# A cross attention's second input, loaded a second time as columns instead of being turned on TensorE

## The chip, the cores and the metric

The kernel runs on one NeuronCore of a Trainium2 chip. Its time is the device time of one execution in microseconds (us); less is better. All arithmetic is in float32, in places split in two float32r parts, as told below.

## The reference, cut to what matters

Two transformer layers follow each other on 256 rows of 1024 numbers. The second has a cross attention whose keys and values come from a second input `mem` (256 rows of 1024 numbers), not from the running rows. Only this part is touched:

```python
def _rmsnorm(x, g):
    x32 = x.astype(jnp.float32)
    y = x32 * lax.rsqrt(jnp.mean(x32 * x32, axis=-1, keepdims=True) + EPS)
    return y.astype(x.dtype) * g

def _cross_attention(hn, memn, wq, wkv, wo):
    B, L, _ = hn.shape
    q = (hn @ wq).reshape(B, L, X_HEADS, X_HEAD_DIM)
    kv = memn @ wkv
    k, v = jnp.split(kv, 2, axis=-1)
    k = k.reshape(B, N_MEM, X_HEADS, X_HEAD_DIM)
    v = v.reshape(B, N_MEM, X_HEADS, X_HEAD_DIM)
    s = jnp.einsum('bshd,bmhd->bhsm', q.astype(jnp.float32), k.astype(jnp.float32)) * (X_HEAD_DIM ** -0.5)
    p = jax.nn.softmax(s, axis=-1)
    o = jnp.einsum('bhsm,bmhd->bshd', p.astype(v.dtype), v).reshape(B, L, X_W)
    return o @ wo
...
    h = h + _cross_attention(_rmsnorm(h, norm_x_g[l]), _rmsnorm(mem, norm_mem_g[l]),
                             wx_q[l], wx_kv[l], wx_o[l])
```

The norm of a row of `mem` is a factor of that row (one number for each of the 256 rows) times a gain for each column. The keys and the values are linear in the normed row, so the row's factor can be put on `mem` or on the finished keys and values.

## The kernel before, in words

**Weights.** Every matrix product streams its weights from HBM in units of 128 x 1024 numbers (512 KB). SyncE's queue (SP) loads a unit into one of five buffers `raw`; ScalarE (ACT) rounds it to float32r in `whi` (line 940, through `make_hi`); VectorE (DVE) puts the rest, raw less hi, in `wlo` (line 1452, `make_lo`); TensorE (PE) multiplies hi by hi, lo by hi and hi by lo into PSUM (`pb`), three matmuls for each product. Each of `raw`, `whi` and `wlo` has five buffers. `make_hi` of a unit waits until PE is done with the unit five before it, the load of a unit waits for `make_lo` of the unit five before it. PE takes 12 matmuls of 512 columns for a unit of the form `rows`, and 24 of 256 columns for one of the form `cols`.

**Order.** Each engine has a program of its own, written out by hand; semaphores tie them together. `run(name, side, ...)` of ACT and DVE makes the units of one weight group and after each unit takes one step of the side programs given to it, which hold the work that does not follow the stream of weights. PE's `rows` and `cols` do the same: behind each unit comes one step of a side program. The groups in question, in order: `b1_wa`, `b1_wb` (branches of the first layer), `b1_wo` (its output product), `f1_up`/`f1_dn` (its feed forward), then `mk` and `mv` (keys and values of the cross attention, from `mem`), then `b2_cg0` and what follows in the second layer. The side program `turn_block1` runs beside `b1_wb1`, `b1_wo0`, `b1_wo1` and the first `f1_up`.

**mem.** SP waits until the first layer's attention is done (`pv_done`), since `MEM` lies where that attention's tiles were, and then loads `MEM`, 256 rows as two tiles of 128 rows. ACT squares and sums the rows (line 985), DVE makes the mean (`mean`, lines 1482 and 1484), GpSimd (POOL) the factor by a power (line 2144), and DVE multiplies the rows by it (`norm_rows`, line 1494: four instructions of 512 columns). In `turn_block1` PE turns the scaled rows into columns: `turn_tiles(T_MEM, j, MEM, ...)` for j = 0 to 3, four 128 x 128 transposes each (line 418 is the source of each transpose, line 414 of each matmul), into PSUM bank 4 + j. ACT copies them with the gain into `OT` (a part of `ZO`) rounded to float32r, DVE puts the rest beside it (line 1511). Much later `mk` makes the keys, columns of `KXT`, and `mv` the values, `VX`, which ACT copies out of PSUM; the cross attention uses both.

The first layer's own input takes another way, with lines that the change uses again: its factor is put on a diagonal (`DR`, line 1946), one matmul of `ones` with it spreads the factors over all partitions, and DVE copies them to `RX` (line 1950).

Of the kernel before, what the change touches and what calls it, by code (L numbers as in the profile page):

```python
# [8 lines left out]
F32 = mybir.dt.float32  # L9
F32R = mybir.dt.float32r  # L10
ALU = mybir.AluOpType
# [3 lines left out]
P = 128  # L15
# [24 lines left out]
POW = {n: i for i, n in enumerate((N_X, N_MEM, N_MIX, N_XA, N_END))}  # L40

END_PARTS = (((0, 1, 0, 512), (1, 1, 512, 1024)), ((0, 2, 0, 320), (1, 2, 640, 1024), (0, 3, 320, 640)))
SCALED = {n: i for i, n in enumerate((N_MEM, N_MIX))}
GAIN = {T_X: "norm1", T_MEM: "normmem", T_2: "norm2", T_MIX: "normmix", T_XA: "normx", T_FFN: "normffn"}
PE_CONV = 5

# [1 line left out]
def build(nc, A, out):  # L48
    ctx = ExitStack()
    with ctx:  # L50
# [54 lines left out]
        DR = work(W0 + 15224, "DR", 256)  # L105
        RX = work(W0 + 18296, "RX", 256)
        MEM = work(W0 + 10480, "MEM", 2048)
        MSQ = work(W0 + 8192, "MSQ", 1024)
        RT = work(W0 + 8704, "RT", 512)[:, :].rearrange("p (i n) -> p i n", i=2)
        HF = work(W0 + 9216, "HF", 1024)[:, :].rearrange("p (i n) -> p i n", i=4)  # L110
# [171 lines left out]

        x_in, mem_in = [sem("x_landed0"), sem("x_landed1")], [sem("mem_landed0"), sem("mem_landed1")]
        xt_in, gain_in = [sem(f"x_columns_landed{i}") for i in range(3)], sem("first_gain_landed")
        dr_made, rx_done, rx_out = sem("factor_diagonals"), sem("factor_rows"), sem("factor_rows_copied")
        cst_in, prm_in, cb_in, wc_in = sem("consts_landed"), sem("params_landed"), sem("consts2_landed"), sem("wcmp_landed")
        zeros, first_in, first_k = sem("zeros_made"), sem("first_k_tile_landed"), sem("first_k_tile_made")
# [59 lines left out]
        def sync_program(e):  # L347
# [28 lines left out]
            for u in range(NRAW, NU):  # L376
                if u == 8:
                    e.dma_start(WC, A["wcmp"].rearrange("p (w j e) -> p w j e", w=2, j=16)).then_inc(wc_in, 16)
                if u == 12:
                    e.dma_start(CB[:, :], A["consts2"]).then_inc(cb_in, 16)  # L380
                if u == b1 + 46:
                    e.wait_ge(pv_done, 16)
                    for t in range(2):
                        e.dma_start(MEM[:, t * D:t * D + D], memv[:, t, :]).then_inc(mem_in[t], 16)
                for k, (at, name) in enumerate(((48, "b2_q1"), (58, "b2_gc0"), (62, "b2_gc1"), (66, "b2_ga0"))):
                    if u == b2 + at:
                        e.wait_ge(*out_at[name, 3 if k == 0 else 1])
                        src = A["b_gate_2"][:, 512 * k:512 * k + 512].broadcast_to([P, 512])
                        e.dma_start(BG[:, :], src).then_inc(bg_in, 16)
                if u == b2 + 28:  # L390
                    e.wait_ge(*out_at["b2_ca1", 3])
                    e.wait_ge(u4_zero, 1)
                if b2 + 28 <= u < b2 + 32:
                    j = u - b2 - 28
                    a = 1 if j == 0 else 0
                    for g in range(4):
                        e.dma_start(U4[32 * j:32 * j + 32, :, g, a:284],
                                    U2[32 * g:32 * g + 32, PE_CONV:8, j + a - 1:j + 283]).then_inc(u4_in, 16)
                if u == f2 + 24:
                    e.wait_ge(xv_done, 4)  # L400
                    e.dma_start(GF[:, :], A["norm_final_g_2"].broadcast_to([P, D])).then_inc(gf_in, 16)
                e.wait_ge(lo, u - NRAW + 1)
                load(u)
# [8 lines left out]
        def tensor_program(e):  # L412
# [122 lines left out]
                for _ in steps:  # L535
                    pass

            def rows_scaled(n, j):
                e.wait_ge(scaled, 4 * SCALED[n] + 2 * (j // 2) + 2)

            def factor_rows():
                yield
# [6 lines left out]
            def turn_block1():  # L549
                yield  # L550
                for j in range(2):
                    e.wait_ge(mixed, 2)
                    turn_tiles(T_M1, j, GB)
                    yield
                yield
                for j in range(2, 4):
                    e.wait_ge(mixed, 4)
                    turn_tiles(T_M1, j, GB)
                yield
                for j in range(4):  # L560
                    rows_scaled(N_MEM, j)
                    turn_tiles(T_MEM, j, MEM, (t_lo, t_at[T_M1, j]))
                    yield
                for j in range(2):
                    e.wait_ge(*out_at["b1_wo0", 1])
                    turn_tiles(T_2, j, X, (t_lo, t_at[T_MEM, j]))
                    yield
                yield
                for j in range(2, 4):
                    e.wait_ge(*out_at["b1_wo1", 1])  # L570
                    turn_tiles(T_2, j, X, (t_lo, t_at[T_MEM, j]))
                yield

            def turn_mix():
                for _ in range(3):
                    yield
                for j in range(4):
                    rows_scaled(N_MIX, j)
                    turn_tiles(T_MIX, j, XS, out_at[f"f1_dn7_{j // 2}", j % 2])
                yield  # L580

# [293 lines left out]
            def cross_scores(h):  # L875
                o = PB[4 + h]
                e.wait_ge(t_lo, t_at[T_XA, h])
                e.wait_ge(*out_at["xq", h])
                for t in range(2):
                    i = mm(o[:, 256 * t:256 * t + 256], QX[:, h, t * P:t * P + P], KXT[:, h, :], t == 0, t == 1)  # L880
                i.then_inc(xs_done, 1)
# [50 lines left out]
        def scalar_program(e):  # L932
# [56 lines left out]
                return XS[:, t * D + 512 * i:t * D + 512 * i + 512]  # L989

            def make_t_hi(s, j, T):
                e.wait_ge(turned, 4 * (s - 1) + j + 1)
                if s in GAIN:
                    for k in range(2):
                        kt = 2 * j + k
# [6 lines left out]
            def turn_block1():  # L1002
# [6 lines left out]
                for j in range(2, 4):  # L1009
                    make_t_hi(T_M1, j, XT)  # L1010
                yield
                for j in range(4):
                    make_t_hi(T_MEM, j, OT)
                    yield
                for j in range(2):
                    make_t_hi(T_2, j, XT)
# [316 lines left out]
                make_t_hi(T_MIX, j, XT)  # L1333
            run("mv")
            for t in range(2):
                copy_out("mv", t, VX[:, t, :])


            run("b2_cg0")
# [92 lines left out]
        def vector_program(e):  # L1432
# [85 lines left out]
                                    d[:, :, 0, :].bitcast(F32), ALU.subtract).then_inc(t_lo, 1)  # L1518

            def turn_block1():  # L1520
                yield
                yield
                for j in range(2):
                    make_t_lo(T_M1, j, XT)
                    yield
                yield
                for j in range(2, 4):
                    make_t_lo(T_M1, j, XT)
                yield
                for j in range(4):  # L1530
                    make_t_lo(T_MEM, j, OT)
                    yield
                for j in range(2):
                    make_t_lo(T_2, j, XT)
                    yield
                yield
                for j in range(2, 4):
                    make_t_lo(T_2, j, XT)
                yield
# [259 lines left out]
            def attention2():  # L1799
                for s in range(45):  # L1800
# [36 lines left out]
                        make_o_lo(h, 4 + h, 6)  # L1837
                    yield

            def conv_blocks():  # L1840
                for n in range(8 - PE_CONV):
                    e.tensor_tensor(WQ[n].rearrange("p q g c -> p (q g) c"),
# [142 lines left out]
            for i in range(2):  # L1985
                run(f"b1_wa{i}")
                times(f"b1_wa{i}", GA, i, gate_made(0))
            norm_rows(N_MEM, MEM, MEM)
            run("b1_wb0")
            times("b1_wb0", GB, 0, gate_made(2), N_X)  # L1990
            plus("b1_wb0", GB, 0, GA)
# [13 lines left out]
            run("mk")  # L2005
            for j in range(4):
                make_t_lo(T_MIX, j, XT)
            run("mv", conv_blocks())


            step(e.memset(U2[:, :, 0:30], 0.0))
# [244 lines left out]
```

## Time and profile before

| | |
|---|---|
| median of three runs | 939.59 us (939.23 to 940.73) |
| the profiled execution | 939.12 us, of which its span in the trace is 937.3 us |
| TensorE busy | 923.2 us (98% of the span) |
| VectorE busy | 681.2 us (73%) |
| ScalarE busy | 520.1 us (55%) |
| GpSimd busy | 14.9 us (2%) |
| read from HBM | 163.72 MB, 176 GB/s over the span |
| granted TensorE clock | 0.999 of full speed |

The profile is one execution. Its span runs from the first to the last instruction; the execution's own time is 1.8 us more. Busy time is the sum of instruction durations; a matmul's duration begins before the one ahead of it has ended, so the distance between the starts of two matmuls tells what one costs in a stream, and its duration does not.

### The profile page before, as it was taken

Reading aid. Unit: us, or ns where it says so; the run is one execution under the profiler, and the core shown is the slowest. Engines: PE = TensorE matmul, PEld = TensorE weight load, DVE = VectorE, ACT = ScalarE, POOL = GpSimd, SP = SyncE. Lnnn points to the kernel's source line nnn. Section 1 sums busy time; section 2 is a strip of 40 time slices with the busy share of each in tenths; the row PEclk is TensorE's granted clock in tenths of the full one; section 3 lists DMA queues with packets and bytes.
Section 4 is the critical chain, followed back from the end, with each engine's and each line's share of the span. In section 5 each row is a group of like instructions: output and inputs, shape, how many; then the busy total and the mean of one; then the engine's idle time right before and its main releaser. Section 6 shows DMA issues by size and latency. Waiting matters only on the chain.

```text
span 937.3 us, 14384 instructions
## 1 busy us (share of the span) xinstructions
PE 923.2 (98%) x5515; PEld 795.0 (85%) x5515; DVE 681.2 (73%) x1173; ACT 520.1 (55%) x880; POOL 14.9 (2%) x20
## 2 busy tenths in 40 slices
PE   8999999999999999999999999999999999999997
PEld 6898987788888888889999988887788888888886
DVE  5769975477776666667478989999786676666665
ACT  5745677745654444456444436654945664454553
POOL 0300000000000000000000000000000000000000
PEclk9999999999999999999999999999999999999999
DMA  9855444656565566554654945554465346655551
GB/s 347 284 151 155 136 139 133 201 186 183 172 204 196 185 188 193 185 198 141 208 161 142 248 136 154 171 173 155 157 229 175 94 159 222 214 189 180 180 180 45
DMA packets 89315, 167.51 MB, mean 179 GB/s; under 512 B 7648, under 2 KB 11808, under 8 KB 89120
## 3 DMA queue, kind: packets, MB, share of 16 engines
q1 hardware_dynamic: 89024, 166.53, 56.1%
q8 instruction: 44, 0.72, 0.3%
q14 instruction: 23, 0.19, 0.1%
q10 hardware_dynamic: 224, 0.07, 0.0%
HBM read 163.72 MB, written 1.05 MB: 176 GB/s over the span
## 4 chain that ended last, share of the span: by engine, by line
PE 92%; ACT 3%; DVE 2%; DMA 2%; issue 1%; SPq 0%; POOL 0%; POOLq 0%; DVEq 0%
PE pb L414 89%; PE pb L418 3%; DMA raw<-in_w_in 2%; ACT whi L940 1%; DVE wlo L1452 1%; ACT YC L1252 0%; DVE LNS L1878 0%; ACT XS L985 0%; ACT ZO L940 0%; ACT GA L1075 0%; ACT L1252 0%; ACT L1075 0%; DVE GA L1739 0%; DVE ST L1614 0%; ACT S L1389 0%
## 5 line engine op out<-in xcount | busy, mean ns | idle before, releaser
L1452 DVE TENSOR_TENSOR wlo<-raw,whi 128x1024 fp32r<-128x1024 f32 (+2 forms) x300 | 357.0, 1213 | 148.3 <-ACT whi L940 147.0
L940 ACT ACTIVATE whi<-raw 128x1024 fp32r<-128x1024 f32 (+2 forms) x302 | 309.8, 1045 | 164.3 <-PE pb L414 151.0
L414 PE MATMUL pb<-XT,whi 128*128 128x256 f32 (+1 forms) x1552 | 372.6, 323 | 1.3 <-issue 1.3
L414 PE MATMUL pb<-XT,wlo 128*128 128x256 f32 (+1 forms) x1032 | 290.5, 282 | 0.0
L414 PEld LDWEIGHTS pb<-XT,whi 128*128 128x128 f32 x1552 | 257.6, 190 | 29.6 <-issue 5.3
L414 PE MATMUL pb<-whi,ZO 128*128 128x512 f32 (+1 forms) x808 | 253.1, 390 | 0.4 <-DVE wlo L1452 0.4
L414 PEld LDWEIGHTS pb<-XT,wlo 128*128 128x128 f32 (+1 forms) x1032 | 195.8, 190 | 0.5
L414 PE MATMUL pb<-whi,XT 128*128 128x512 f32 (+1 forms) x544 | 176.4, 394 | 4.1 <-DVE wlo L1452 2.8
L414 PEld LDWEIGHTS pb<-whi,ZO 128*128 128x128 f32 x808 | 151.2, 188 | 33.1 <-DVE wlo L1452 1.6
L414 PE MATMUL pb<-wlo,ZO 128*128 128x512 f32 (+1 forms) x404 | 156.5, 387 | 0.0
L414 PEld LDWEIGHTS pb<-whi,XT 128*128 128x128 f32 x544 | 101.2, 188 | 26.7 <-DVE wlo L1452 4.3
L414 PE MATMUL pb<-wlo,XT 128*128 128x512 f32 (+1 forms) x272 | 103.2, 385 | 0.0
L414 PEld LDWEIGHTS pb<-wlo,ZO 128*128 128x128 f32 x404 | 75.9, 188 | 14.8
L1865 DVE SCALAR_TENSOR_TENSOR YC<-U,PR,YC 128x256 f32<-128x256 f32 x150 | 63.4, 477 | 0.0
L414 PEld LDWEIGHTS pb<-wlo,XT 128*128 128x128 f32 x272 | 51.3, 188 | 8.8
L940 ACT ACTIVATE RT<-pb 128x256 f32<-128x256 f32 x64 | 24.1, 376 | 40.5 <-PE pb L414 40.5
L1779 DVE TENSOR_TENSOR HF<-pb,RT 128x256 f32<-128x256 f32 x64 | 26.8, 418 | 24.8 <-ACT RT L940 24.8
L940 ACT ACTIVATE ZO<-HF 128x256 fp32r<-128x256 f32 x64 | 26.8, 418 | 24.9 <-DVE HF L1782 23.3
L1141 ACT ACTIVATE SM<-SM,ST 128x128 f32<-128x128 f32 (+1 forms) x48 | 21.4, 447 | 16.7 <-DVE ST L1593 16.7
L1782 DVE SCALAR_TENSOR_TENSOR HF<-HF 128x256 f32<-128x256 f32 x64 | 27.2, 425 | 2.2
L1771 DVE TENSOR_TENSOR ZO<-HF,ZO 128x256 fp32r<-128x256 f32 x64 | 26.8, 419 | 2.4 <-ACT ZO L940 0.6
L2144 POOL TENSOR_TENSOR ST<-ST,CST 128x1 f32<-128x1 f32 (+3 forms) x14 | 13.5, 971 | 917.9 <-DVE ST L1484 687.5
(220 smaller groups left out, 593.7 us busy)
## 6 DMA issues: line engine op xcount, KB each, us to landing
raw<-in_w_in SPq DMA_DIRECT2D x107, 512.0 KB, 3.7
raw<-in_w_ff SPq DMA_DIRECT2D x64, 512.0 KB, 4.5
raw<-in_w_up SPq DMA_DIRECT2D x32, 512.0 KB, 4.4
raw<-in_w_down SPq DMA_DIRECT2D x32, 512.0 KB, 4.6
raw<-in_w_branch_b SPq DMA_DIRECT2D x8, 512.0 KB, 4.8
raw<-in_w_out SPq DMA_DIRECT2D x8, 512.0 KB, 4.8
raw<-in_wx_kv SPq DMA_DIRECT2D x8, 512.0 KB, 4.2
raw<-in_w_attn_out SPq DMA_DIRECT2D x8, 512.0 KB, 3.4
```

The lines of the kernel that those rows point to most:

```text
L414: return e.matmul(o, l, r, start=start, stop=stop, skip_group_check=True)
L418: return e.transpose(o, s, ident[0:n, 0:n])
L940: return e.activation(o, i, ACT.Copy, scale=scale)
L1141: i = e.activation(SM[j % 4][:, c0:c1], SM[j % 4][:, c0:c1], ACT.Exp, bias=INM[j % 4][:, t:t + 1], scale=post, accum_out=ISM[j % 4][:, t:t ...
L1452: e.tensor_tensor(wlo[u % NW][:, 0:c], raw[u % NRAW][:, 0:c], whi[u % NW][:, 0:c].bitcast(F32), ALU.subtract).then_inc(lo, 1)
L1771: e.tensor_tensor(ZT[:, a + 256:a + 512], HF[:, f, :], ZT[:, a:a + 256].bitcast(F32), ALU.subtract).then_inc(h_lo, 1)
L1779: e.tensor_tensor(HF[:, f, :], PB[bank_of[name, f]][:, 0:256], RT[:, m % 2, :], ALU.add).then_inc(out_d, 1)
L1782: e.scalar_tensor_tensor(out=HF[:, f, :], in0=HF[:, f, :], scalar=0.0, in1=HF[:, f, :], op0=ALU.max, op1=ALU.mult).then_inc(h_sq, 1)
L1865: m = e.scalar_tensor_tensor(out=YC[:, f, :], in0=U2[:, f, k:k + 256], scalar=prm("convw2", 8 * k + f), in1=YC[:, f, :], op0=ALU.mult, op1 ...
L2144: return e.tensor_tensor(dst, src, mhalf(rows, n), ALU.pow)
```

## The change

`mem` is loaded once more, already turned by the host: `memt` holds its columns as rows of the tile `MT` (128 x 2048, 1 MB), which lies where the first layer's queries, keys and values were. SP issues this load between the same wait and the two loads of `MEM`. ACT and DVE read `MT` for the two parts of `OT`, with the gain and without the row's factor. `MEM` is still loaded for the squares; it isn't scaled and isn't turned any more. The row's factor now goes on the results: on the keys by a multiply in place (`scale_keys`, with the factors spread over partitions by one matmul and a copy to `RX`), on the values as the scale of ACT's copy out of PSUM. A table of turn numbers (`TURN`) replaces arithmetic, since one turn fewer is counted. The pieces below are, in order: the tile's place; SP's loads; PE's `turn_block1` and `cross_scores`; ACT's `turn_block1` and its copy behind `mv`; DVE's `turn_block1` (two pieces), the new `scale_keys`, and the calls ahead of `b1_wb0` and at `mv`.

```diff
+        MT = work(W0, "MT", 2048)
...
                 if u == b1 + 46:
                     e.wait_ge(pv_done, 16)
+                    e.dma_start(MT[:, :], A["memt"]).then_inc(mt_in, 16)
                     for t in range(2):
                         e.dma_start(MEM[:, t * D:t * D + D], memv[:, t, :]).then_inc(mem_in[t], 16)
...
-                for j in range(4):
-                    rows_scaled(N_MEM, j)
-                    turn_tiles(T_MEM, j, MEM, (t_lo, t_at[T_M1, j]))
-                    yield
+                e.wait_ge(t_lo, t_at[T_M1, 0])
+                e.wait_ge(dr_made, 4)
+                mm(PB[4][:, 0:256], ones, DR[:, :], True, True).then_inc(rx_done, 1)
+                for _ in range(4):
+                    yield
+                e.wait_ge(rx_out, 2)
                 for j in range(2):
                     e.wait_ge(*out_at["b1_wo0", 1])
-                    turn_tiles(T_2, j, X, (t_lo, t_at[T_MEM, j]))
+                    turn_tiles(T_2, j, X, (t_lo, t_at[T_M1, j]))
...
                 e.wait_ge(*out_at["xq", h])
+                e.wait_ge(kx_scaled, 4)
...
+                e.wait_ge(mt_in, 16)
+                e.wait_ge(*tile_at["b1_wa1", 1])
                 for j in range(4):
-                    make_t_hi(T_MEM, j, OT)
+                    for kt in (2 * j, 2 * j + 1):
+                        copy(OT[:, kt * 512:kt * 512 + 256], MT[:, kt * 256:kt * 256 + 256],
+                             prm(GAIN[T_MEM], kt)).then_inc(t_hi, 1)
                     yield
...
             for t in range(2):
-                copy_out("mv", t, VX[:, t, :])
+                e.wait_ge(factor, 2 * POW[N_MEM] + t + 1)
+                copy_out("mv", t, VX[:, t, :], NR[N_MEM][t])
...
+                for t in range(2):
+                    e.wait_ge(factor, 2 * POW[N_MEM] + t + 1)
+                    e.tensor_scalar(DR[:, t * P:t * P + P], ident, NR[N_MEM][t], None, ALU.mult).then_inc(dr_made, 1)
...
+                e.wait_ge(rx_done, 2)
+                e.tensor_copy(RX[:, :], PB[4][:, 0:256]).then_inc(rx_out, 1)
                 for j in range(4):
-                    make_t_lo(T_MEM, j, OT)
+                    for kt in (2 * j, 2 * j + 1):
+                        a = kt * 512
+                        e.wait_ge(t_hi, t_at[T_MEM, j] - 1 + kt % 2)
+                        e.scalar_tensor_tensor(out=OT[:, a + 256:a + 512], in0=MT[:, kt * 256:kt * 256 + 256],
+                                               scalar=prm(GAIN[T_MEM], kt), in1=OT[:, a:a + 256].bitcast(F32),
+                                               op0=ALU.mult, op1=ALU.subtract).then_inc(t_lo, 1)
                     yield
...
+            def scale_keys():
+                for f in range(4):
+                    e.wait_ge(*out_at["mk", f])
+                    if f == 0:
+                        e.wait_ge(rx_out, 2)
+                    e.tensor_tensor(KXT[:, f, :], KXT[:, f, :], RX[:, :], ALU.mult).then_inc(kx_scaled, 1)
+                    yield
...
-            norm_rows(N_MEM, MEM, MEM)
+            for t in range(2):
+                mean(N_MEM, t, 4 * N_MEM + 3 + t)
...
-            run("mv", conv_blocks())
+            run("mv", conv_blocks(), scale_keys())
```

Where PE turned `mem`, beside the product `b1_wo0`, its program of before reads as follows; `pb<-CST,MEM x4` is one `turn_tiles` of `mem`, the matmuls between are one weight unit:

```order
789 L414 MATMUL pb<-whi,XT 128x512
790 L418 MATMUL pb<-CST,MEM 128x128 x4
791 L414 MATMUL pb<-whi,XT 128x512
792 L414 MATMUL pb<-wlo,XT 128x512
...
799 L414 MATMUL pb<-whi,XT 128x512
800 L418 MATMUL pb<-CST,MEM 128x128 x4
```

The same place in the changed program (its line numbers are 4 higher); `pb<-DR,CST` is the one matmul that spreads the factors:

```order
789 L418 MATMUL pb<-whi,XT 128x512
790 L418 MATMUL pb<-DR,CST 128x256
791 L418 MATMUL pb<-whi,XT 128x512
792 L418 MATMUL pb<-wlo,XT 128x512
...
799 L418 MATMUL pb<-whi,XT 128x512 x2
800 L418 MATMUL pb<-wlo,XT 128x512
```

Of the four groups of four transposes none is left; one matmul stands at the place of the first, and the other three places hold nothing.

On DVE, the program of before around `mv`, behind `mk`; `wlo` is `make_lo`, `WQ` a table for the second layer's convolution, `U` a memset:

```order
341 L1452 TENSOR_TENSOR wlo<-raw,whi 128x1024
342 L1842 TENSOR_TENSOR WQ<-CST,PR 128x1024
343 L1452 TENSOR_TENSOR wlo<-raw,whi 128x1024
344 L1842 TENSOR_TENSOR WQ<-CST,PR 128x1024
345 L1452 TENSOR_TENSOR wlo<-raw,whi 128x1024
346 L1842 TENSOR_TENSOR WQ<-CST,PR 128x1024
347 L1452 TENSOR_TENSOR wlo<-raw,whi 128x1024
348 L2011 MEMSET U 128x8x30
349 L1452 TENSOR_TENSOR wlo<-raw,whi 128x1024 x8
```

The same place of the changed program:

```order
343 L1463 TENSOR_TENSOR wlo<-raw,whi 128x1024
344 L1873 TENSOR_TENSOR WQ<-CST,PR 128x1024
345 L1868 TENSOR_TENSOR KXT<-KXT,RX 128x256
346 L1463 TENSOR_TENSOR wlo<-raw,whi 128x1024
347 L1873 TENSOR_TENSOR WQ<-CST,PR 128x1024
348 L1868 TENSOR_TENSOR KXT<-KXT,RX 128x256
349 L1463 TENSOR_TENSOR wlo<-raw,whi 128x1024
350 L1873 TENSOR_TENSOR WQ<-CST,PR 128x1024
351 L1868 TENSOR_TENSOR KXT<-KXT,RX 128x256
352 L1463 TENSOR_TENSOR wlo<-raw,whi 128x1024
353 L1868 TENSOR_TENSOR KXT<-KXT,RX 128x256
354 L2043 MEMSET U 128x8x30
```

Three of the four multiplies of the keys now stand ahead of a `make_lo`, and one behind the last.

## Rows read from the trace of the kernel before

**Rows 1.** Page, busy time of each engine, and the chain by engine.

```profile
PE 923.2 (98%) x5515; PEld 795.0 (85%) x5515; DVE 681.2 (73%) x1173; ACT 520.1 (55%) x880; POOL 14.9 (2%) x20
...
PE 92%; ACT 3%; DVE 2%; DMA 2%; issue 1%; SPq 0%; POOL 0%; POOLq 0%; DVEq 0%
```

**Rows 2.** PE timeline, turns of mem: start us, us, engine, line, op, count.

```profile
223.79 0.60 PE L418 MATMUL pb<-CST,MEM 128*128 128x128 f32 x4
...
236.61 0.60 PE L418 MATMUL pb<-CST,X 128*128 128x128 f32 x4
```

**Rows 3.** PE timeline, a stretch of 114 matmuls with no turn.

```profile
184.30 0.62 PE L414 MATMUL pb<-whi,ZO 128*128 128x512 f32 x2
...
210.14 0.62 PE L414 MATMUL pb<-whi,ZO 128*128 128x512 f32 x2
```

**Rows 4.** PE timeline, a float32 matmul of ones inside the stream.

```profile
656.26 0.39 PE L414 MATMUL pb<-whi,ZO 128*128 128x512 f32 x1
656.49 0.59 PE L414 MATMUL pb<-LNS,CST 128*128 128x256 f32 x2
...
657.15 0.40 PE L414 MATMUL pb<-wlo,ZO 128*128 128x512 f32 x1
```

**Rows 5.** Groups by shape, 20-50 and 223.79-236.61 us: xcount, busy us, mean ns, idle.

```profile
L414 PE MATMUL pb<-DR,CST 128*128 128x256 f32 x2 | 0.6, 377 | 0.0
...
L1946 DVE TENSOR_SCALAR DR<-CST,ST 128x128 f32<-128x128 f32 x2 | 0.6, 286 | 0.1
...
L418 PE MATMUL pb<-CST,MEM 128*128 128x128 f32 x16 | 2.4, 272 | 0.0
```

**Rows 6.** DMA issues: KB each, median us to landing.

```profile
raw<-in_w_in SPq DMA_DIRECT2D x107, 512.0 KB, 3.7
...
MEM<-in_mem SPq DMA_DIRECT2D x2, 512.0 KB, 6.5
...
raw<-in_w_branch_b SPq DMA_DIRECT2D x1, 512.0 KB, 7.1
...
WC<-in_wcmp SPq DMA_DIRECT2D x1, 1024.0 KB, 11.1
```

**Rows 7.** SP and ACT timelines, loads of mem and their use.

```profile
177.83 0.82 SPq L384 DMA_DIRECT2D MEM<-in_mem  x2
179.33 13.51 SPq L356 DMA_DIRECT2D raw<-in_w_branch_b  x6
...
189.54 1.06 ACT L940 ACTIVATE whi<-raw 128x1024 fp32r<-128x1024 f32 x1 [1.66 <-PE pb L414]
190.51 0.61 ACT L985 ACTIVATE MSQ<-MEM 128x512 f32<-128x512 f32 x1
...
203.14 1.06 ACT L940 ACTIVATE whi<-raw 128x1024 fp32r<-128x1024 f32 x1 [1.66 <-PE pb L414]
```

**Rows 8.** DVE timeline, from the scaling to the diagonals' place.

```profile
196.54 1.84 DVE L1494 TENSOR_SCALAR MEM<-MEM,ST 128x512 f32<-128x512 f32 x4 [0.41 <-POOL ST L2144]
198.29 4.62 DVE L1452 TENSOR_TENSOR wlo<-raw,whi 128x1024 fp32r<-128x1024 f32 x4
...
207.67 3.49 DVE L1452 TENSOR_TENSOR wlo<-raw,whi 128x1024 fp32r<-128x1024 f32 x3
```

**Rows 9.** ACT, DVE and PE timelines, at mv.

```profile
440.35 1.06 ACT L940 ACTIVATE whi<-raw 128x1024 fp32r<-128x1024 f32 x1 [0.96 <-PE pb L414]
...
444.35 1.22 DVE L1452 TENSOR_TENSOR wlo<-raw,whi 128x1024 fp32r<-128x1024 f32 x1
...
445.53 0.40 PE L414 MATMUL pb<-XT,whi 128*128 128x256 f32 x2
...
446.60 0.40 PE L414 MATMUL pb<-XT,whi 128*128 128x256 f32 x2
```

**Rows 10.** Groups by shape, whole span: a DVE multiply of 256 columns.

```profile
L1724 DVE TENSOR_TENSOR CC<-pb,RX 128x256 f32<-128x256 f32 x8 | 2.8, 415 | 0.0
```

**Rows 11.** Page, PE's longest idle time with no releaser.

```profile
L414 PE MATMUL pb<-XT,whi 128*128 128x256 f32 (+1 forms) x1552 | 372.6, 323 | 1.3 <-issue 1.3
```

More of the change, by code:

```diff
@@ L42 @@
 END_PARTS = (((0, 1, 0, 512), (1, 1, 512, 1024)), ((0, 2, 0, 320), (1, 2, 640, 1024), (0, 3, 320, 640)))
-SCALED = {n: i for i, n in enumerate((N_MEM, N_MIX))}
+TURN = {s: i for i, s in enumerate((T_M1, T_2, T_MIX, T_M2, T_XA, T_FFN))}
 GAIN = {T_X: "norm1", T_MEM: "normmem", T_2: "norm2", T_MIX: "normmix", T_XA: "normx", T_FFN: "normffn"}
@@ L284, in build @@
         xt_in, gain_in = [sem(f"x_columns_landed{i}") for i in range(3)], sem("first_gain_landed")
+        mt_in, kx_scaled = sem("mem_columns_landed"), sem("cross_keys_scaled")
         dr_made, rx_done, rx_out = sem("factor_diagonals"), sem("factor_rows"), sem("factor_rows_copied")
@@ L536, in now, with rows_scaled @@
                     pass
-            def rows_scaled(n, j):
-                e.wait_ge(scaled, 4 * SCALED[n] + 2 * (j // 2) + 2)
+            def rows_scaled(j):
+                e.wait_ge(scaled, 2 * (j // 2) + 2)
             def factor_rows():
@@ L570, in turn_block1 @@
                     e.wait_ge(*out_at["b1_wo1", 1])
-                    turn_tiles(T_2, j, X, (t_lo, t_at[T_MEM, j]))
+                    turn_tiles(T_2, j, X, (t_lo, t_at[T_M1, j]))
                 yield
@@ L577, in turn_mix @@
                 for j in range(4):
-                    rows_scaled(N_MIX, j)
+                    rows_scaled(j)
                     turn_tiles(T_MIX, j, XS, out_at[f"f1_dn7_{j // 2}", j % 2])
@@ L991, in make_t_hi @@
             def make_t_hi(s, j, T):
-                e.wait_ge(turned, 4 * (s - 1) + j + 1)
+                e.wait_ge(turned, 4 * TURN[s] + j + 1)
                 if s in GAIN:
@@ L2242 @@
     xt = I["x"].reshape(256, 8, P).transpose(2, 1, 0).reshape(P, 2048)
-    arrays = {"xt": xt, "params": params, "consts": c, "consts2": c2, "wcmp": wcmp, "x": I["x"], "mem_2": I["mem_2"],
+    memt = I["mem_2"].reshape(256, 8, P).transpose(2, 1, 0).reshape(P, 2048)
+    arrays = {"xt": xt, "memt": memt, "params": params, "consts": c, "consts2": c2, "wcmp": wcmp, "x": I["x"], "mem_2": I["mem_2"],
               "b_gate_2": I["b_gate_2"], "norm_final_g_2": I["norm_final_g_2"].reshape(1, D)}
```

## The prediction

> **What bounds the kernel now.** I read the page first: PE is busy for 923.2 of 937.3 us, and the chain that ended last runs 92% through it, against 3% through ACT and 2% through DVE [rows 1]. So a microsecond taken off PE's stream is worth a microsecond, and work added to ACT, DVE or the loads is worth nothing until it makes PE wait. Then the timelines around the places that the change touches, to see two things: what the turned tiles of mem cost in the stream, and how far ahead of PE the other engines run there. In the stretch of the turns [rows 2] the rows carry no idle time ahead of any instruction of PE.
>
> **What PE loses.** Sixteen transposes, in four groups. From the first group's start to the start of the next turn behind the fourth is 236.61 - 223.79 = 12.82 us, for four units of twelve matmuls and four groups [rows 2]. The same matmuls without turns: 114 in 210.14 - 184.30 = 25.84 us, 0.2267 us each, so 2.72 us a unit and 10.88 us for four [rows 3]. The four groups cost 12.82 - 10.88 = 1.94 us, 0.49 us each, the slower start of the matmul behind each included.
>
> The transposes' own durations would give more: 272 ns each [rows 5], 4.35 us for 16. But each starts before the one ahead has ended, so I go by the distances, 1.94 / 16 = 0.12 us each. The Trainium skill, "TensorE: Matmul & The Clock Gate", section "Part 4: PE-mode transpose", gives about 275 ns for a 128 x 128 transpose in a kernel's context (measured in bf16); an estimate by it takes 16 x 0.275 = 4.4 us off PE where the distances take 1.94.
>
> **What PE gains.** One float32 matmul of ones with the diagonals, 256 columns. The trace has such a matmul, as two rows, inside the stream: the matmul ahead starts at 656.26, the second one behind at 657.15; two steps of 0.2267 from 656.26 would bring that start to 656.71 had the ones not been there, so they cost 0.44 us [rows 4]. Bounds: not below one step of the stream, 0.23 us; not above twice its busy time of 377 ns, 0.75 us [rows 5]. I take 0.44, the only one read in a stream of the same kind. PE also gets a wait on `kx_scaled` at each of four score products and one on `rx_out`; all are met long before (below). Such waits can't be priced from a row; I bound them by 0 and by 0.05 us each, a fifth of one matmul's step, so 0 to 0.25 us, and take 0, because a matmul that waits for several things that are done, the ones of [rows 4] among them, shows no more than its own cost.
>
> So PE's stream gets shorter by 1.94 - 0.44 = 1.50 us.
>
> **What lies beside it, and its cover.**
> *SP and the transfers.* The wait for `pv_done` is the same one; behind it MT, 1 MB, goes out ahead of MEM, and the loads of weights stand behind in the same queue. Before, MEM's two loads went out from 177.83 on and took 6.5 us (median), and the first load of weights behind them, at 179.33, took 7.1 us and landed at 186.4 [rows 6, 7]. One more issue on SP is 0.41 us (two took 0.82), and the next load went out 0.68 us behind those, so SP itself delays nothing. With MEM's 1 MB ahead the weights took 7.1 us where such a load commonly takes 3.7 [rows 6]: 3.4 us for 1 MB. I take the same for MT's 1 MB: MEM lands at 184.3 + 3.4 = 187.7, the weights at 189.8. Lower bound 0; upper bound the 11.1 us that the one other load of 1 MB took from issue to landing, near the kernel's start amid other loads [rows 6].
> What needs them: ACT's `make_hi` of those weights began at 189.54, when PE had freed the buffer, and the squares of MEM at 190.51 [rows 7]. So at 3.4 us ACT waits 0.3 us. PE wants that unit only four units later, at 189.54 + 4 x 2.72 = 200.4; ACT takes 1.06 and DVE 1.2 us for it, so its weights may land at 198.1, a delay of 11.7 us. The next unit's hi stands behind the squares on ACT, its lo behind the means on DVE, from 198.29 to 199.5; PE wants it at 203.1, a slack of 3.6 us, and 5.4 us once the 1.84 us of scaling ahead of it are gone [rows 8]. If DVE took up the means as soon as the squares are there, that path would break when these start at 190.5 + 5.4 = 195.9, a delay of MEM of 11.6 us. So even the upper bound is covered, by half a microsecond.
> *DVE beside b1_wb1.* Two diagonals, 0.57 us together [rows 5], stand behind the first of the three `make_lo`s from 207.67 on. That one's unit was freed for ACT at 203.14, the next one's 2.72 us later, so PE wants the next at 205.86 + 10.88 = 216.7; its lo was done at 207.67 + 2 x 1.16 = 210.0, now 210.6 [rows 7, 8]. Uncovered it would cost its 0.57 us. The factors from POOL were there at 196.5 [rows 8], more than 10 us earlier. Then one copy to RX, taken like the multiply of its size at 0.41 us [rows 10], ahead of the first rest of OT; uncovered again its 0.41. Before, DVE waited just there for ACT's copy of a turned tile; that copy now comes from MT and waits for no turn. PE wants `rx_out` four units later, 11 us on, and `dr_made` 15 us behind the diagonals.
> *DVE at mv.* Four multiplies of 256 columns at 0.415 us [rows 10], 1.66 us. Three stand ahead of the `make_lo` that began at 444.35. Its unit was freed for ACT at 440.35, so PE wants it four units later: two of mv are left behind the one that it then begins, and end when cg0 starts at 445.53; two units of cg0 (24 matmuls of 0.12 us, 2.88 us each) bring 451.3 [rows 9]. Lo was done at 445.57, now 1.25 us later at 446.8: 4.5 us are left. If that cover were gone the cost would be at most the 1.66 us. The loads that wait for these `make_lo`s go out up to 1.25 us later and land in some 4 us, into buffers that ACT wants only when PE has freed the unit five before, 10.9 us after `make_hi` of it could begin.
> *ACT.* As many copies, read from MT instead of PSUM. The two copies of the values get a factor as an operand instead of a constant; the banks that they free are wanted by the third and the fourth tile of cg0, not by the first, so a tenth of a microsecond there moves nothing.
>
> **Sum.** The profiled execution was 939.12 us, so 937.62 for such a one. The median of the runs is 0.47 us above it; I put the same on top: 938.1 us, 0.16% less. Before the end nothing brings the 1.5 us back: the later waits of PE are for engines that PE itself paces, so they move with it.
>
> **The rivals.**
> *Durations rule (faster).* If a transpose costs its duration, PE loses 4.35 us and gains 0.75 by the same rule: 3.6 us net, 936.0. For it speaks only the mean duration [rows 5]; against it the distances [rows 2, 3]. An estimate by the skill's 275 ns, in the page named above, is 4.4 - 0.44 = 4.0 us, 935.6. 5%.
> *A stall of code (either way).* PE has one gap of 1.3 us with no releaser anywhere [rows 11]. It lies ahead of the change, but PE's program is shorter behind it, and a gap of this kind could come or go. Gone, or the ones hidden to their lower bound together with a lucky median: 938.1 - 1.3 = 936.8, 12%. One more: 939.4, 13%, which with my sum is as good as no change.
> *The loads (slower).* MT ahead of MEM and the weights, in one queue. It decides from a delay of 11.7 us on (11.6 for MEM); each microsecond more is one of PE, first at the unit wanted at 200.4. Slower than before begins at 11.7 + 1.5 = 13.2 us; at 16 us it gives 938.1 + 4.3 = 942.4. For it: MEM and the weights behind already took 6.5 to 7.1 us where 3.7 is common. Against: 1 MB took at most 11.1 us, from issue to landing, amid the loads of the start [rows 6]. 4%.
> *It brings nothing because a wait takes its place.* PE would wait at T_2's turns for `rx_out`, or DVE for the ones: 939.6. Against: 11 us of slack. Within the 13% above.
>
> **How the numbers follow.** Forecast 66%, and for itself 937.6 to 938.7: ones 0.23 to 0.75, waits 0 to 0.25, and some 0.3 us for a median of three. This measurement tells a change of 0.2%, 1.88 us, from none, so the line for faster is at 937.7 and my forecast lies 0.4 us on the near side of it: of its 66% I give 8 to faster. Faster: 5 + 12 + 8 = 25%. Slower, beyond 941.5: 4%, and 1 for what I didn't think of. Same: 70%. The range reaches to the two stalls: 936.8 to 939.5.
>
> **What the changed profile would show.** On PE, between the turns of GB and those of X, units 2.72 us apart with one pair of rows `pb<-DR,CST`; from that pair to the first turn of X 11.3 us where 12.8 were. If it is more than 11.6, the ones were mis-sized. No idle PE time at 200 to 204 us nor at 443 to 452; MEM's loads landing near 188 and ACT's squares starting where they did, or there is my error on the transfers. All later stages, the first of them f1_up, 1.5 us earlier and no more, until the end. The prediction is wrong if a distance that holds before doesn't hold after: if PE shows a wait for `wlo` or `whi` that was not there, or the 2.72 us don't come back.

## The result, and the profile after

The changed kernel takes 938.05 us (median of 22 runs, 937.48 to 939.74) where the kernel before takes 939.5 us (22 runs on the same chip, 939.08 to 941.17): 1.45 us less, a ratio of 0.9983 with a 95% interval of 0.9977 to 0.999. The profiled execution took 937.61 us, its span in the trace 935.8 us. By the bound of 0.2% that is no change, though the whole interval lies below 1; in microseconds it reaches from 0.9 to 2.2 less.

The page's busy times and its chain by engine, to be set against [rows 1]:

```profile
PE 922.6 (99%) x5501; PEld 794.4 (85%) x5501; DVE 681.6 (73%) x1176; ACT 520.4 (56%) x880; POOL 15.5 (2%) x20
...
PE 92%; ACT 3%; DVE 2%; DMA 2%; issue 1%; SPq 0%; POOL 0%; POOLq 0%; DVEq 0%
```

The bound has not moved. PE's records are 14 fewer: 16 transposes gone, and one float32 matmul, which stands as two records, come. PE's timeline at the change, between the turns of `GB` and those of `X`:

```profile
220.06 1.03 PE L422 MATMUL pb<-CST,GB 128*128 128x128 f32 x8
...
223.67 0.59 PE L418 MATMUL pb<-DR,CST 128*128 128x256 f32 x2
...
235.04 0.60 PE L422 MATMUL pb<-CST,X 128*128 128x128 f32 x4
```

From the place of the first turn of mem to the first turn of `X` there are 235.04 - 223.67 = 11.37 us; before it was 12.82 [rows 2]. So 1.45 us are gone here. Absolute times of two executions differ a little from the start on (the matmul at the change starts 0.12 us earlier here, and in other executions below up to 1.8 us later, of which the last section explains 1.6), so I compare distances. For the stretch from the turns of `GB` on, the kernel before has one more row:

```profile
220.18 1.03 PE L418 MATMUL pb<-CST,GB 128*128 128x128 f32 x8
```

That is 236.61 - 220.18 = 16.43 us before and 235.04 - 220.06 = 14.98 after, 1.45 again. Runs below are read by this same distance.

Next, SP, ACT and DVE after, to be set against [rows 7, 8]; first SP's timeline.

```profile
177.71 0.34 SPq L386 DMA_DIRECT2D MT<-in_memt  x1
178.09 0.91 SPq L388 DMA_DIRECT2D MEM<-in_mem  x2
179.22 13.51 SPq L359 DMA_DIRECT2D raw<-in_w_branch_b  x6
```

DMA issues between 176 and 200 us (KB each, median us to landing):

```profile
MEM<-in_mem SPq DMA_DIRECT2D x2, 512.0 KB, 9.2
```

ACT's timeline:

```profile
189.44 1.07 ACT L947 ACTIVATE whi<-raw 128x1024 fp32r<-128x1024 f32 x1 [1.67 <-DMA raw<-in_w_branch_b]
190.41 0.61 ACT L992 ACTIVATE MSQ<-MEM 128x512 f32<-128x512 f32 x1
```

`MEM` took 9.2 us where it took 6.5. ACT's `make_hi` began 0.10 us earlier than before, but what ended its wait is now the load of the weights, and before it was PE [rows 7]: the transfer has eaten its slack on ACT to the last tenth, and costs nothing. DVE's timeline:

```profile
208.69 0.48 DVE L1535 TENSOR_SCALAR DR<-CST,ST 128x128 f32<-128x128 f32 x2
...
224.30 0.42 DVE L1546 COPY RX<-pb 128x256 f32<-128x256 f32 x1 [0.21 <-PE pb L418]
...
443.47 0.42 DVE L1868 TENSOR_TENSOR KXT<-KXT,RX 128x256 f32<-128x256 f32 x1
443.81 1.22 DVE L1464 TENSOR_TENSOR wlo<-raw,whi 128x1024 fp32r<-128x1024 f32 x1
...
445.90 3.53 DVE L1464 TENSOR_TENSOR wlo<-raw,whi 128x1024 fp32r<-128x1024 f32 x3 [0.29 <-ACT whi L947]
```

DVE's new work is all there and none of it shows on PE. The `make_lo` behind the third multiply of the keys starts at 443.81 where it started at 444.35 [rows 9]; with everything 1.5 us earlier it is 1.0 us late by its own stage, and behind the two short instructions that follow it DVE waits for ACT again.

### The profile page after: what moved, and what is told of

Read it like the earlier page. It is cut to its first block, busy times and chain, and to the rows that moved or that the text cites. A ratio compares the mean times of both kernels' runs of the same rounds, so it can differ in the third digit from the quotient of the medians.

```text
span 935.8 us, 14361 instructions
## 1 busy us (share of the span) xinstructions
PE 922.6 (99%) x5501; PEld 794.4 (85%) x5501; DVE 681.6 (73%) x1176; ACT 520.4 (56%) x880; POOL 15.5 (2%) x20
## 4 chain that ended last, share of the span: by engine, by line
PE 92%; ACT 3%; DVE 2%; DMA 2%; issue 1%; SPq 0%; POOL 0%; POOLq 0%; DVEq 0%
PE pb L418 90%; PE pb L422 2%; DMA raw<-in_w_in 2%; ACT whi L947 1%; DVE wlo L1464 1%; ACT YC L1263 0%; DVE LNS L1909 0%; ACT XS L992 0%; ACT ZO L947 0%; ACT GA L1086 0%; ACT L1263 0%; ACT L1086 0%; DVE GA L1761 0%; DVE ST L1636 0%; ACT S L1401 0%
```

## The experiments

The theory: the whole gain is PE's stream between the turns of `GB` and those of `X`, 16 transposes less and one float32 matmul more, and the loads and DVE's work are covered. The rivals: transposes and the ones are priced by their durations; the added load or DVE's work costs something, and the transposes brought more; the gain is partly chance of another program. All medians are set against the kernel before, run between them on the same chip: 939.47 us for the first four, 939.46 for the next four, 939.30 for the last four. Where two experiments are compared, their medians are. The changed kernel took 937.90 us in the first group and 937.97 in the last; the middle group has no run of it and is set against 937.90, since the medians of the kernel before agree to 0.01 us.

**The changed kernel again.**

> The changed kernel itself, beside the same runs of the kernel before as the three below, so that they can be set against it. Theory (only PE's stream counts): 1.5 us less than the kernel before. Rival (part of the 1.5 us is another start of the program): the first turn of X at another time than 1.45 us earlier counted from the matmul of ones.

937.90 us, 1.57 less than before. The first turn of `X` stands 235.27 - 223.91 = 11.36 us behind the ones. The 11.4 us are the program's, not one execution's.

**Transposes added.** In PE's `turn_block1`, behind the ones:

```diff
-                for _ in range(4):
+                yield
+                e.wait_ge(t_lo, t_at[T_M1, 1])
+                for n in (1, 4, 16):
+                    for _ in range(n):
+                        turn(PB[5][:, 0:P], ident)
                     yield
```

> The changed kernel with 21 transposes of the identity added in PE's stream beside b1_wo0, their results unused: 1 behind the first unit, 4 behind the second, 16 behind the third. Theory (distance between starts, 0.12 us each): 2.5 us more than the changed kernel, that is 1.0 us more than the kernel before; the group of 4 takes 0.49 us and that of 16 takes 1.9. Rival (the durations, 0.272 us each): 5.7 us more than the changed kernel, 4.2 more than before; the group of 16 takes 4.4.

940.41 us, 2.51 more than the changed kernel. PE's timeline:

```profile
227.18 0.27 PE L422 MATMUL pb<-CST 128*128 128x128 f32 x1
...
230.03 0.60 PE L422 MATMUL pb<-CST 128*128 128x128 f32 x4
...
233.24 1.91 PE L422 MATMUL pb<-CST 128*128 128x128 f32 x16
...
237.76 0.60 PE L422 MATMUL pb<-CST,X 128*128 128x128 f32 x4
```

A unit of twelve matmuls is 2.72 us [rows 3]. The distances are 2.85, 3.21 and 4.52 us, so 1, 4 and 16 transposes cost 0.13, 0.49 and 1.80 us: 0.11 to 0.13 each, however many. The durations rule is refuted; it wanted 4.4 for the 16.

**Matmuls of ones added.** At the same place:

```diff
...
+                for n in (1, 2, 4):
+                    for _ in range(n):
+                        mm(PB[5][:, 0:256], ones, DR[:, :], True, True)
                     yield
```

> The changed kernel with seven more float32 matmuls of ones with the diagonals (256 columns), results unused: 1, 2 and 4 behind the three units beside b1_wo0. Theory (0.44 us each in a stream): 3.1 us more than the changed kernel, 1.6 more than before. Rivals: one step of the stream each, 0.23: 1.6 more than the changed one; the busy time, 0.75 each: 5.3 more. If the cost is mostly in going from one kind of matmul to the other, the four in a row cost clearly less than 4 x 0.44 = 1.8 us.

941.01 us, 3.11 more than the changed kernel. PE's timeline, each float32 matmul as two records:

```profile
228.68 0.59 PE L418 MATMUL pb<-DR,CST 128*128 128x256 f32 x2
...
231.88 1.02 PE L418 MATMUL pb<-DR,CST 128*128 128x256 f32 x4
...
235.51 1.89 PE L418 MATMUL pb<-DR,CST 128*128 128x256 f32 x8
...
239.98 0.27 PE L422 MATMUL pb<-CST,X 128*128 128x128 f32 x1
```

Less 2.72 each: 0.48 for one, 0.91 for two, 1.75 for four. So it is some 0.43 us each and up to 0.05 more for the first; going from one kind of matmul to the other can cost no more than that 0.05.

**The factors through DRAM, without PE.** PE's ones, DVE's diagonals and its copy to `RX` for mem are left out, and SP stores the factors to DRAM, where the output comes later, and loads them back spread over the partitions, ahead of two later loads of weights:

```diff
+                if u == b1 + 62:
+                    e.wait_ge(factor, 2 * POW[N_MEM] + 2)
+                    for t in range(2):
+                        e.dma_start(out[0, 0:1, t * P:t * P + P].rearrange("o (p n) -> (o p) n", n=1), NR[N_MEM][t]).then_inc(fr_out, 16)
+                if u == b1 + 68:
+                    e.wait_ge(fr_out, 32)
+                    e.dma_start(RX[:, :], out[0, 0:1, 0:256].broadcast_to([P, 256])).then_inc(fr_in, 16)
```

> The changed kernel without the matmul of ones, the diagonals and the copy for mem: SP stores the 256 factors to DRAM (where the output comes later) some 16 units on and loads them back to RX on all partitions 6 units later, long before mv. The computation is the same. Theory (the ones cost PE 0.44 to 0.49 us and all that replaces them is hidden): 0.45 us less than the changed kernel, 1.95 less than before. Rival (the 256 pieces of 4 bytes hold up the loads of weights behind them in SP's queue): PE waits for whi or wlo near 240 us and the time is that of the changed kernel or more.

937.64 us, 0.26 less than the changed kernel. PE's timeline:

```profile
220.17 1.03 PE L430 MATMUL pb<-CST,GB 128*128 128x128 f32 x8
...
234.67 0.60 PE L430 MATMUL pb<-CST,X 128*128 128x128 f32 x4
```

14.50 us, 0.48 less than the 14.98 of the changed kernel, and 1.93 less than the 16.43 of before: the last number is the price of the sixteen turns of mem alone. PE waits for nothing new. DMA issues between 205 and 265 us, the load back and the stores in pieces of 4 bytes:

```profile
RX<-out SPq DMA_DIRECT2D x1, 128.0 KB, 4.2
out<-ST SPq DMA_DIRECT2D x2, 0.5 KB, 8.6
```

Since the median showed less than the trace, it ran again:

> The kernel that passes mem's factors through DRAM, again, beside the changed kernel, since 0.26 us was seen where 0.45 was expected and the intervals are wider than either. Theory: 0.45 us less than the changed kernel. Rival (part of the gain is eaten somewhere): 0.2 us or less.

> The changed kernel beside the three others of this group. Theory: 1.5 us less than the kernel before.

937.51 us against 937.97 for the changed kernel beside it: 0.46 less (ratios to the kernel before 0.9979, 0.9971 to 0.9988, and 0.9984, 0.9975 to 0.9992). The stretch from `GB` to `X` is 236.44 - 221.95 = 14.49 us. The traces show 0.48 and 0.49; the medians show 0.26 and 0.46, and their intervals overlap. This is the fastest version here, by what the stretch says.

**The covered work alone.** The kernel before, with its turns and its scaling, plus the load of `MT`, two diagonals and a copy on DVE, and four multiplies of 256 columns at `mv`, results unused (shortened):

```diff
+                    e.dma_start(MT[:, :], A["memt"]).then_inc(mt_in, 16)
...
+                for t in range(2):
+                    step(e.tensor_scalar(DR[:, t * P:t * P + P], ident, NR[N_MEM][t], None, ALU.mult))
...
+                e.tensor_copy(RX[:, :], DR[:, :])
...
+                    e.tensor_tensor(SCR[:, 256 * f:256 * f + 256], KXT[:, f, :], RX[:, :], ALU.mult)
```

> The kernel before, turns of mem and scaling of its rows kept, with the work added that the change puts beside the stream: the load of MT (1 MB, not used), the two diagonals and a copy of 256 columns to RX on DVE beside b1_wb1, and four multiplies of 256 columns on DVE at mv with results unused. Theory (all of it is covered): 0.0 us against the kernel before. Rival (some of it costs, and the transposes brought more than 1.94): up to 2.6 us more, the sum of the DVE work, or a wait of PE for wlo at 443 to 452 us or for whi at 200 to 204.

939.49 us, 0.03 more than before, ratio 1.0001 (0.9992 to 1.001). PE's waits by releaser (us in total, times, longest) hold nothing that was not there before:

```profile
PE pb L418 <- DVE wlo L1456: 3.2, 3, 1.8
...
PE pb L418 <- ACT whi L944: 0.4, 1, 0.4
```

The stretch from `GB` to `X` is 236.78 - 220.35 = 16.43 us, as before. The cover held for the load and DVE's work together, and here DVE still scales the rows of `mem` besides, so the transposes cannot have brought more than the stretch shows. ACT's copies out of `MT` are not in this run; for them speaks only that PE waits for nothing new in the changed kernel.

**The load made larger.** Between the load of `MT` and those of `MEM`, the same 1 MB again, two times (the first two lines), and then four times with a wait between the pairs (all five):

```diff
+                    e.dma_start(ML[0][:, :], A["memt"]).then_inc(more_in, 16)
+                    e.dma_start(ML[1][:, :], A["memt"]).then_inc(more_in, 16)
+                    e.wait_ge(more_in, 32)
+                    e.dma_start(ML[0][:, :], A["memt"]).then_inc(more_in, 16)
+                    e.dma_start(ML[1][:, :], A["memt"]).then_inc(more_in, 16)
```

> The changed kernel with two more loads of mem's columns (1 MB each, into unused room) between the load of MT and those of MEM. Theory (3.1 to 3.4 us of delay for 1 MB, decides from 11.7 us of delay on): the first weights behind land 3 x 3.1 = 9.3 to 10.2 us later than before, near 196; no PE wait there; same time as the changed kernel, 1.5 less than before. ACT's squares of MEM start near 194. Rival (the cover is thinner): 1 us or more over the changed kernel and PE waiting at 200 to 206 us.

937.95 us, 0.05 from the changed kernel. ACT's timeline: the weights come 8.7 us later than the 186.4 of before, 2.9 us for each MB, and PE waits nowhere in the stretch.

```profile
195.10 1.06 ACT L951 ACTIVATE whi<-raw 128x1024 fp32r<-128x1024 f32 x1 [6.92 <-DMA raw<-in_w_branch_b]
196.07 0.61 ACT L996 ACTIVATE MSQ<-MEM 128x512 f32<-128x512 f32 x1
```

> The changed kernel with four more such loads, the last two behind a wait of SP for the first two (the same room), which costs SP some 2 us more. Theory: delay of the weights behind of 5 x 3.1 + 2 = 17.5 us, so that they land near 204; past the 11.7 us by 5.8, so PE waits 5 to 7 us from 198 to 206 us on and the time is 4 to 5.5 us over the kernel before. Rival (loads catch up or the cover is thicker): under 1.5 us more than the changed kernel.

944.35 us (median of 5 runs): 4.9 over before, as expected, but not by the expected way. ACT's timeline:

```profile
201.57 1.06 ACT L954 ACTIVATE whi<-raw 128x1024 fp32r<-128x1024 f32 x1 [13.45 <-DMA raw<-in_w_branch_b]
```

PE's timeline:

```profile
200.17 0.39 PE L425 MATMUL pb<-whi,ZO 128*128 128x512 f32 x1
203.94 0.80 PE L425 MATMUL pb<-whi,ZO 128*128 128x512 f32 x1 [3.38 <-DVE wlo L1471]
204.53 0.63 PE L425 MATMUL pb<-wlo,ZO 128*128 128x512 f32 x1
204.96 1.05 PE L425 MATMUL pb<-whi,ZO 128*128 128x512 f32 x2
...
209.65 0.39 PE L425 MATMUL pb<-wlo,ZO 128*128 128x512 f32 x1
```

The delay was 15.2 us, not 17.5, and PE started its unit 3.5 us late (203.94 instead of 0.23 behind the matmul at 200.17), not 5 to 7. But then its matmuls stood 0.43 us apart until 209.65: 13 of them in 5.71 us, for which 2.95 would do. The table by stretch shows why. Its columns are the stretch, its length, the busy time of PE, PEld, DVE, ACT and POOL, the granted clock, the share of the DMA engines, GB/s:

```profile
200.00:202.00 2.00, 0.56 (x3) 0.13 (x1) 0.00 (x0) 0.43 (x1) 0.00 (x0) 1.00 1.06 401
202.00:204.00 2.00, 0.06 (x1) 0.06 (x1) 1.34 (x2) 2.00 (x6) 0.00 (x0) 0.70 1.04 389
204.00:206.00 2.00, 2.00 (x5) 1.61 (x6) 1.52 (x6) 2.00 (x6) 0.58 (x2) 0.50 1.08 382
...
210.00:212.00 2.00, 2.00 (x11) 1.65 (x10) 1.44 (x2) 0.58 (x1) 0.00 (x0) 1.00 0.97 352
```

The granted clock fell while PE was still idle (0.70 on average between 202 and 204). After 3.4 us of idleness PE came back at 0.50, 1.2 GHz, and had 2.4 GHz again before 210. 3.5 us late and 2.8 us at half clock make 6.3 of the 6.4 us over the changed kernel.

> As the run with four more loads, but the last of them of half the size, to bring the delay of the weights down by half of 2.9 us. There PE waited 3.38 us at 203.94 and the granted clock then stood at half for some 5 us, so that 6.4 us were lost for 3.4 of waiting. Here PE should wait about 1.9 us at the same place. Theory (a wait this short leaves the clock alone, as the one of 2.77 us did): 1.9 us over the changed kernel, 0.4 over the kernel before. Rival (the clock falls here too): 4.5 to 5 us over the changed kernel.

943.43 us, but in seven runs from 940.63 to 943.96, not around one value. The profiled execution, one of the long ones, waited 2.71 us and not 1.9:

```profile
204.67 0.74 PE L425 MATMUL pb<-whi,ZO 128*128 128x512 f32 x1 [2.71 <-DVE wlo L1471]
```

The table by stretch:

```profile
206.00:208.00 2.00, 2.00 (x6) 1.57 (x5) 1.50 (x5) 2.00 (x3) 1.08 (x2) 0.50 1.04 379
208.00:210.00 2.00, 2.00 (x9) 1.60 (x9) 2.00 (x3) 1.60 (x2) 0.00 (x0) 0.96 0.50 90
```

Here the clock fell after 2.7 us of idleness. But not all that this execution lost was lost here: its granted clock had fallen once before, near 31 us, far ahead of the added loads.

```profile
30.00:34.00 4.00, 4.00 (x12) 3.07 (x12) 2.00 (x4) 0.69 (x1) 3.07 (x2) 0.58 0.84 259
```

Set matmul by matmul against the profiled execution of the changed kernel beside it (938.10 us), it lost 1.6 us from 30 to 35 us, 2.9 at the wait and 1.8 at half clock behind it; it had been 0.4 us ahead, so 5.9 in all. The two short runs, 940.63 and 940.88, lie 2.7 and 2.9 us over the changed kernel, as much as such a wait alone costs, and that of 942.38 lies 4.4 over it, near the wait and its half clock; but they have no trace. The run was to separate a wait from its consequence at 1.9 us and did not: it took half a megabyte off, and the wait came down by 0.7 only.

**DVE's work at mv made larger.** Three multiplies of 1024 columns ahead of each multiply of the keys:

```diff
+                    for i in range(3):
+                        if i or f:
+                            after_step()
+                        step(e.tensor_tensor(SCR[:, :], X[:, 0:D], X[:, D:2 * D], ALU.mult))
```

> The changed kernel with three more multiplies of 1024 columns on DVE ahead of each of the four multiplies of the keys at mv, results unused, some 1.2 us each: nine of them, 10.8 us, stand ahead of the make_lo that had 4.5 us left. Theory: PE waits 6.3 us or somewhat more (the last three stand ahead of the next make_lo, which is then late too: 10 us at most) for wlo from 451 us on; 5 to 8.5 us over the kernel before. Rival (no cover at mv, each us of DVE is one of PE): 14.4 us over the changed kernel. Rival (cover far larger): under 2 us over the changed kernel.

947.17 us (median of 4 runs), 9.3 over the changed kernel, 7.7 over before. PE's timeline:

```profile
449.97 0.50 PE L419 MATMUL pb<-XT,whi 128*128 128x256 f32 x2 [2.77 <-DVE wlo L1465]
...
456.23 0.80 PE L419 MATMUL pb<-XT,whi 128*128 128x256 f32 x2 [3.13 <-DVE wlo L1465]
456.82 0.41 PE L419 MATMUL pb<-XT,wlo 128*128 128x256 f32 x1
...
461.56 0.50 PE L419 MATMUL pb<-XT,whi 128*128 128x256 f32 x2 [0.97 <-DVE wlo L1465]
```

DVE's timeline:

```profile
454.96 1.22 DVE L1465 TENSOR_TENSOR wlo<-raw,whi 128x1024 fp32r<-128x1024 f32 x1
```

The `make_lo` that had 4.5 us left ended at 456.18, 11.15 us later than the 445.03 of the changed kernel, and PE took up its unit 456.23 - 449.74 = 6.5 us late (cg0's first matmul at 443.98 in the changed kernel, and two units of 2.88). So 4.7 us were covered; that the two executions stand some 0.2 us apart from the start on is in both numbers and drops out. The third wait adds 1.1 us, and the clock, granted at 0.50 between 456 and 458 us, 1.3: the twelve matmuls from 456.23 on took 2.73 us, for which 1.44 would do. That makes 8.9 of the 9.3. After the first wait, of 2.77 us, the matmuls stood 0.12 apart: the clock had not fallen.

**Matmuls ahead of a wait.** Three more matmuls of ones at the first layer's place:

```diff
+                for _ in range(3):
+                    mm(PB[4][:, 0:256], ones, DR[:, :], True, True)
                 mm(PB[4][:, 0:256], ones, DR[:, :], True, True).then_inc(rx_done, 1)
```

> The changed kernel with three more float32 matmuls of ones, results unused, at the first layer's own place for them (near 27.3 us), where PE waits 1.75 us for wlo three matmuls later, at 29.62. Theory (what stands ahead of a wait costs nothing until the wait is used up): 3 x 0.44 = 1.3 us less waiting at 29.6, and the time of the changed kernel, 1.5 us less than before. Rival (the price of a matmul is the same anywhere): 1.3 us over the changed kernel.

937.87 us, 0.1 less than the changed kernel beside it. PE's next matmul, in the changed kernel and then here:

```profile
29.62 0.50 PE L418 MATMUL pb<-whi,XT 128*128 128x512 f32 x1 [1.75 <-DVE wlo L1464]
```

```profile
27.50 1.89 PE L418 MATMUL pb<-DR,CST 128*128 128x256 f32 x8
29.87 0.50 PE L418 MATMUL pb<-whi,XT 128*128 128x512 f32 x1 [0.48 <-DVE wlo L1466]
```

The wait fell by 1.27 us, 0.42 for each matmul added. Where PE waits anyway they are free.

## Why the prediction was right, step by step

The forecast was 938.1 us and 937.62 for the profiled execution; measured were 938.05 and 937.61. The steps hold one by one, so the 0.05 us of the sum is not luck of opposite errors. That both times agree to some hundredths is luck: the interval of the measured gain is 1.2 us wide, the profiled execution stood 0.12 us earlier before the change was reached, and an execution with a fall of the clock near 31 us (last section), as 5 of the 22 probably had, takes 1.6 us more. The prediction named nothing that shifts executions by so much except its gap with no releaser, and that did not move.

*The turns, 1.94 us.* Right: 1.93 by the kernel without turns or ones, and 0.13, 0.49 and 1.80 for 1, 4 and 16 added ones. The 275 ns that the Trainium skill gives in "TensorE: Matmul & The Clock Gate", section "Part 4: PE-mode transpose" (measured in bf16), agrees with the duration that this trace gives (272 ns in float32, [rows 5]). A duration does not tell what a transpose costs in this stream.

*The ones, 0.44 us.* 0.48: the only mis-sized term of the sum, by 0.04. The two rows that I took it from [rows 4] stand between matmuls of the same kind, so I cannot say what makes the difference.

*The added waits, 0 to 0.25, taken as 0.* PE's total wait for each engine is within 0.1 us of before, but for ACT's `whi`: 0.4 us here and 1.3 before. It is 0.4 too in the kernel before with the covered work, which is no faster for it, so the change did not bring that.

*The transfers, covered, 3.4 us for 1 MB, deciding from 11.7 us on.* The price was 2.9 to 3.0 us, so 3.4 was too much, and nothing hung on it. The predicted wait of ACT for the weights, 0.3 us, is not in the trace: buffer and weights come at the same time. The point of decision was right to 0.2 us: with 15.2 us of delay PE was 3.5 late, and 15.2 - 11.7 = 3.5. The second limit, squares of MEM at 195.9, was not seen to cost at 196.07, but that is too close to it to say much. What was wrong in that rival is its price, "each microsecond more is one of PE": the first 3.5 cost 6.4, since the clock fell.

*DVE at mv, late 1.25, 4.5 left.* It was 1.0 late after the shift, and 4.7 of cover by the run that used it up. *DVE beside b1_wb1, 0.57 and 0.41 covered.* Right, by the run with the covered work alone.

*The offset of 0.47 us from profiled execution to median.* 0.44.

Of the rivals the durations rule is refuted by both runs that added instructions. The stall of code did not come: 1.3 us with no releaser before, 1.3 after. That a program's length can bring one is neither shown nor excluded. A wait in the place of the turns did not come. The chances as written add up to 101 and not 100: with 66 for the forecast, of which 8 go to faster, and 13 for one more gap, `same` comes to 71.

## What to carry to other kernels

Price an instruction of a busy PE by the distance between starts with and without it, at a place of the same kind: here that gave the total to 0.05 us, where the durations would have said 3.6 instead of 1.45. Ask of each instruction whether PE waits behind it anyway: the same matmul was worth 0.48 us at 224 us and nothing at 27. And where a cover breaks count the clock too: 3.5 us of lateness cost 6.3, and 2.9 cost 4.6, though one wait of 2.77 us cost no more than itself.

## What the hardware showed that I had not expected

The granted clock after a wait of PE: in the added waits, idle for 0.97 us and 2.77 us it stayed at 2.4 GHz, and after 2.71, 3.13 and 3.38 us PE ran at 1.2 GHz for 3 to 6 us. And a shorter wait, which both kernels have, went both ways too. It is that of 1.8 us near 28 us; here it is in the second run of the factors through DRAM:

```profile
29.92 0.50 PE L426 MATMUL pb<-whi,XT 128*128 128x512 f32 x1 [1.79 <-DVE wlo L1468]
```

The table by stretch from 30 to 34 us, in that execution and then in the changed kernel's beside it:

```profile
30.00:34.00 4.00, 4.00 (x13) 3.18 (x14) 2.18 (x4) 0.69 (x1) 3.20 (x2) 0.68 0.76 242
```

```profile
30.00:34.00 4.00, 3.87 (x20) 3.37 (x21) 2.38 (x5) 1.52 (x4) 3.42 (x3) 1.00 0.70 225
```

In three of the fourteen profiled executions (the matmuls of ones, the 4.5 MB, and this one) the clock was down to 0.50 for some 3 us from about 31 us on, 0.9 to 1.5 us after PE was back from the same wait of 1.8 us; in the eleven others, ten of them with that wait, it stood at 1.00 throughout these 4 us. It cost 1.6 us: from the matmul behind the wait to the one behind the gap with no releaser there are 54.9 us here and 53.3 beside it. No distance that I used above holds this place.

This probably is why the times of one kernel fall into two groups: before, 16 runs from 939.08 to 939.91 and 6 from 940.68 to 941.17; changed, 17 from 937.48 to 938.31 and 5 from 939.13 to 939.74, these 5 with a granted clock of 0.997 over the span and the 17 with 0.998 or more. Of most long runs there is no trace, so that is not shown for each. Nor is it shown that a shorter wait prevents it: with the wait down to 0.48 us none of eleven runs was long, but neither was one of the eleven of the changed kernel beside it.

The stores of 256 factors as pieces of 4 bytes, 8.6 us to landing, held nothing up that PE wanted.
